# Gaps behind streamed weight blocks: where the matmul's moving operand begins within 512 bytes

## The reference

```python
h = rms_norm_2(x, attn_norm[l])
proj = h @ w_in[l]                         # 3648 columns
...                                        # three attention mixers
x = x + mixed @ w_o[l]
h = rms_norm_2(x, mlp_norm[l])
x = x + jnp.square(jax.nn.relu(h @ w_up[l])) @ w_down[l]   # 8192 wide
```

## Time and profile before

| | |
|---|---|
| Median of three runs | 3000.07 us |
| The profiled execution's own time | 3000.52 us |
| Its span | 2998.7 us |
| TensorE busy (matmul) | 2876.8 us, 96% of the span, 13692 matmuls |
| TensorE busy (weight load) | 2424.2 us, 81% |
| VectorE, ScalarE busy | 1878.9 us (63%), 1478.9 us (49%) |
| Loaded by SyncE's queue | 600.42 MB in 170912 packets, 59.3% of 16 engines |

### The profile page before, as it was taken

How to read it: one execution, slowest core, us unless ns; L and a number is a source line. 1 busy time by engine, 2 the same in 40 slices (tenths; PEclk the granted TensorE clock), 3 DMA queues, 4 the chain that set the end, 5 groups by cost and what they waited for, 6 DMA issues and landing times.

```text
span 2998.7 us, 35050 instructions
## 1 busy us (share of the span) xinstructions
PE 2876.8 (96%) x13692; PEld 2424.2 (81%) x13692; DVE 1878.9 (63%) x2387; ACT 1478.9 (49%) x2038; POOL 48.5 (2%) x60
## 2 busy tenths in 40 slices
PE   5998997999999999999999999999999999999998
PEld 4886776888888888788888888888887888888887
DVE  7997998669855557655444554545566554445554
ACT  4446544565546655644334444455546443344443
POOL 0000000000000000000000000000000000000000
PEclk9999998999999999999999999999999999999999
DMA  9994687757654544455555555555445555655654
GB/s 381 341 351 166 222 312 287 271 180 252 229 174 157 175 139 153 171 185 187 190 195 190 184 188 191 182 179 163 140 157 172 186 189 190 192 189 187 201 192 140
DMA packets 173045, 609.66 MB, mean 203 GB/s; under 512 B 19360, under 2 KB 19632, under 8 KB 172240
## 3 DMA queue, kind: packets, MB, share of 16 engines
q1 hardware_dynamic: 170912, 600.42, 59.3%
q0 software_dynamic: 1824, 6.61, 0.8%
q10 hardware_dynamic: 144, 0.39, 0.0%
HBM read 605.24 MB, written 2.10 MB: 203 GB/s over the span
## 4 chain that ended last, share of the span: by engine, by line
PE 83%; DVE 8%; ACT 4%; DMA 3%; issue 2%; SPq 0%; POOL 0%; POOLq 0%; ACTq 0%; DVEq 0%
PE ps L1908 26%; PE ps L1911 25%; PE ps L1915 25%; DVE w_lo L1214 2%; PE ps L1867 2%; DVE raw L1322 1%; PE ps L2033 1%; PE ps L2017 1%; ACT w_hi L876 1%; PE ps L1925 1%; DMA raw<-in_w_ina 1%; ACT probs L1078 1%; DMA raw<-in_w_modT 1%; DMA raw<-in_w_in 0%; DMA raw<-in_w_inc 0%
## 5 line engine op out<-in xcount | busy, mean ns | idle before, releaser
L1214 DVE TENSOR_TENSOR w_lo<-raw,w_hi 128x1024 fp32r<-128x1024 f32 (+4 forms) x988 | 1158.1, 1176 | 967.7 <-ACT w_hi L876 963.7
L876 ACT ACTIVATE w_hi<-raw 128x1024 fp32r<-128x1024 f32 (+4 forms) x988 | 1003.1, 1019 | 1229.2 <-PE ps L1915 1061.8
L1908 PE MATMUL ps<-w_hi,hT_hi 128*128 128x512 f32 (+3 forms) x2848 | 764.0, 390 | 35.2 <-ACT hT_hi L957 18.6
L1911 PE MATMUL ps<-w_lo,hT_hi 128*128 128x512 f32 (+3 forms) x2848 | 740.2, 382 | 0.8 <-DVE w_lo L1214 0.8
L1915 PE MATMUL ps<-w_hi,hT_lo 128*128 128x512 f32 (+3 forms) x2848 | 736.8, 380 | 0.0
L1908 PEld LDWEIGHTS ps<-w_hi,hT_hi 128*128 128x128 f32 x2848 | 519.7, 190 | 126.4 <-issue 25.5
L1911 PEld LDWEIGHTS ps<-w_lo,hT_hi 128*128 128x128 f32 x2848 | 535.1, 190 | 91.7 <-DVE w_lo L1214 1.1
L1915 PEld LDWEIGHTS ps<-w_hi,hT_lo 128*128 128x128 f32 x2848 | 534.3, 189 | 89.2
L1908 PE MATMUL ps<-w_hi,uT_hi 128*128 128x512 f32 x1024 | 275.7, 390 | 0.0
L1911 PE MATMUL ps<-w_lo,uT_hi 128*128 128x512 f32 x1024 | 274.4, 389 | 0.0
L1915 PE MATMUL ps<-w_hi,uT_lo 128*128 128x512 f32 x1024 | 274.4, 389 | 0.0
(11 more groups left out here) (246 smaller groups left out, 1476.1 us busy)
## 6 DMA issues: line engine op xcount, KB each, us to landing
raw<-in_w_up SPq DMA_DIRECT2D x256, 512.0 KB, 3.4
raw<-in_w_down SPq DMA_DIRECT2D x256, 512.0 KB, 3.4
raw<-in_w_modT SPq DMA_DIRECT2D x192, 512.0 KB, 5.5
raw<-in_w_rest SPq DMA_DIRECT2D x80, 456.0 KB, 3.3
raw<-in_w_z SPq DMA_DIRECT2D x64, 512.0 KB, 4.5
raw<-in_w_out SPq DMA_DIRECT2D x64, 512.0 KB, 4.5
raw<-in_w_rest SPq DMA_DIRECT2D x48, 344.0 KB, 3.5
raw<-in_w_oa SPq DMA_DIRECT2D x32, 512.0 KB, 3.4
```

The lines of the kernel that those rows point to most:

```text
L876: act.activation(w_hi[:, L % SPLIT_SLOTS, 0:c, 0:w], blocks(raw, G % RAW_SLOTS, c, w), ACT.Copy).then_inc(S.hi_ready, 1)
L1214: dve.tensor_tensor(blocks(w_lo, r, c, w), blocks(raw, r, c, w), w_hi[:, s, 0:c, 0:w].bitcast(F32), ALU.subtract).then_inc(S.group_read, 1)
L1908: pe.matmul(o, rows(hi, c, t), wh[c], start=start and c == 0, stop=False)
L1911: pe.matmul(o, rows(hi, c, t), wl[:, c], start=False, stop=False)
```

## The change

Each `raw` slot gets 4 unused words behind it (16 bytes), and each block of `w_hi` gets 16 (64 bytes). The places that used a whole slot now name its first 1024 words. Nothing else is edited, but what is allocated behind `raw` moves: `w_hi` by 160 bytes, `hf` and the work area by 672 (160 + 512).

```diff
+RAW_SHIFT = 4
+SHIFT = 16
...
-        raw = sb("raw", [P, RAW_SLOTS, GROUP])
-        w_lo = at("w_lo", [P, RAW_SLOTS, GROUP], F32R, cursor[0] - 4 * RAW_SLOTS * GROUP)
+        raw = sb("raw", [P, RAW_SLOTS, GROUP + RAW_SHIFT])
+        w_lo = at("w_lo", [P, RAW_SLOTS, GROUP + RAW_SHIFT], F32R, cursor[0] - 4 * RAW_SLOTS * (GROUP + RAW_SHIFT))
...
-        w_hi = sb("w_hi", [P, SPLIT_SLOTS, GROUP // COLS, COLS], F32R)
+        w_hi = sb("w_hi", [P, SPLIT_SLOTS, GROUP // COLS, COLS + SHIFT], F32R)
...
-                w = raw[:, G % RAW_SLOTS]
+                w = raw[:, G % RAW_SLOTS, 0:GROUP]
...
-                w = raw[:, G % RAW_SLOTS:G % RAW_SLOTS + 2].rearrange("p s n -> p (s n)")
-                dve.scalar_tensor_tensor(out=w, in0=w, scalar=1.0, in1=c_row[:].rearrange("p a n -> p (a n)"),
+                w = raw[:, G % RAW_SLOTS:G % RAW_SLOTS + 2, 0:GROUP]
+                dve.scalar_tensor_tensor(out=w, in0=w, scalar=1.0, in1=c_row[:],
```

## The result

The changed kernel takes 3043.89 us (median of four runs, 3039.1 to 3045.24), the kernel before 2999.68 on the same chip. The ratio is 1.0143, 95% interval 1.0131 to 1.0155: 1.4% slower, 44 us between the medians. Forecast were 3021 us, with 3007 to 3040 as the forecast's own range and 2935 to 3060 over all cases. The direction held, the amount is twice the forecast one.

The account below looks back on a forecast made before the run. Behind a DMA-paced opening of 225 us, TensorE's matmul step was taken as the bound. 3000.52 us plus 20.5 for 512-wide matmuls, all else 0, gave 3021.0, or 3021 at the runs' median; range 3007 to 3040, over all cases 2935 to 3060.

Parts of the forecast that it names:

- The bound, and the place of the change: Behind the first 225 us, time is the number of matmuls times their step; the 512-wide matmuls' step is what changes.
- The excess of 13.4 ns: Each 512-wide matmul's step over 213.3 ns of array time, taken as TensorE's moving-block and next-stationary-piece reads of SBUF meeting.
- The price per matmul, +2.3 ns: Each of 8892 512-wide matmuls was to take 2.3 ns longer from off-grid starts, +20.5 us in all.
- 344's +6: At width 344, each of the two matmuls off the 512 grid was read as 6 ns longer.
- the unsettled 230: Behind a TensorE pause, aligned blocks take 230 ns each before settling at 226.7; the 3.3 ns difference was noted above +2.3.
- The stationary side: The prediction noted that `uT` moves to 160 bytes past the grid while `hT` stays on it, with no separate price.
- Gaps on ScalarE and VectorE 0: Writing `w_hi` with a gap between its two runs was to cost 0; idle time would hide any step.
- Landings 0: DMA landings off the grid in the first 225 us were taken as 0, with +28 us as the other end.
- Widths 344 to 456 at 0: Some 2900 matmuls of these widths already mix offsets, so the change was to cost them 0.
- Rival 1: Fewer meetings of TensorE's two reads with many offsets, so a smaller excess and a faster kernel: 2970 us, chance 0.33.
- Rival 3: Varied offsets keep TensorE often in the worst phases: +6 ns for each of 8892 matmuls, +56 us, 3056; chance 0.06.
- The signs named: In the "down" products, durations should spread from 389/389/389, median near 391, and four matmuls take 0.91 to 0.93 us.

## Why the prediction was right and wrong

- The bound, and the place of the change: right. TensorE's step sets the time, and 40.8 to 44 of 44.3 us are 512-wide matmuls.
- The excess of 13.4 ns is TensorE's own and comes and goes with the phase of two reads: right as far as it is TensorE's own (alone it is 226.7 too). That one of the two is the data of the next weight load is not borne out, since 2 stationary columns leave 15.6 to 18.3 ns. The stationary piece's start counts; making the piece smaller doesn't lower the excess.
- The price per matmul, +2.3 ns: this step failed. It measured 44 us / 8892 = 5.0 ns. I averaged what off-grid starts did at widths 344 and 456 (2.0) and how far 450 and 456 lie above the settled 512 (2.4 and 2.6). The last two say nothing about starts: alone, with every block aligned, 450 columns take 203.3 ns, just the 203.3 of the earlier trace rows, and 456 take 208.9, 18.9 over the array time.

```profile
374.44 7.57 PE L137 MATMUL ps<-fill 128*128 128x450 f32 x36
381.85 0.30 PE L138 MATMUL ps<-fill 128*128 128x64 f32 x2
```

The 2.0 rests mostly on 344's +6, and 344 alone and aligned settles at 157.8 in one repetition and at 153.3 in the other. So these widths don't settle at 13.4 over even when aligned, and their off-grid blocks had little to lose; what 512 has to lose is its settled state. The trace before had the better row: the unsettled 230 of the earlier trace rows, 3.3 ns, which I named and set aside. Taken over the whole trace, the 871 steps of 512 columns other than 226 or 227 ns average 231.7, and with their neighbours counted in 230.6: 4.9 or 3.8 ns more than the settled step, +34 to +44 us. That is worked out after the fact, but from the trace before alone.
- The stationary side: I let "uT moves to 160 past the grid" stand and gave it no price. Alone it costs 23 us. The starts should have been tabulated against `hT` and `uT` separately.
- Gaps on ScalarE and VectorE 0: right (1058 and 1224 ns for 1024 elements). Landings 0: the opening 225 us moved 350 GB/s against 358, but 353 and 354 also in kernels that leave `raw` alone, and the longer matmuls account for the whole difference; no cost of landings is shown.
- Widths 344 to 456 at 0: nearly. 450 rose from 203.6 to 205.2 and 344 from 155.3 to 157.4, together 2.4 us.
- Rival 1 (fewer meetings), which got 0.33, rested on the idea that an average start is better than the aligned one. None that was measured is better than the aligned one. Rival 3's mark, medians over 394, was met in the low term of the down products (396) without its 56 us: the other two terms lie lower there, with means of 393.
- The signs named: the spread came (387 to 403), the median was 396, not 391, and four matmuls take 0.92 to 0.94 us.

## What to carry to other kernels

Where float32 (fp32r) blocks are streamed through TensorE at full clock, keep the start of the moving block and that of the stationary piece equal modulo 256 bytes: here it is worth 5 ns of 232 for each 512-column matmul, and a pad of 256 is free where one of 64 costs 1.1%. With 512 columns this was tried at equal starts of 0, 64 and 160. Anything allocated in front of them can break it, so the start of the area is as much a part of the layout as the pads. If a trace shows hundreds of matmuls of one and the same duration, that regularity is something that the kernel has and can lose; the same trace's unsettled matmuls, taken all together, give a first price.

## What the runs showed of the hardware

- With the stationary piece on the grid, the step of a 512-column float32 matmul at 2.4 GHz depends on the moving start modulo 256 bytes: 226.7 ns at 0, 228.9 at 64, 230 to 234.7 at the other multiples of 16 up to 224, 236.7 at 240 and at 4. Moving both by 64 or 160 bytes gives 226.7 again, but the difference of the starts is not all: a stationary start of 240 alone leaves 226.7, where the difference gives 231.7. At 1.2 GHz nothing of it is seen: 425 ns for 512 columns before, and a mean of 426.4 ns over 42 such steps in the changed kernel.
- Disturbed, a line of aligned matmuls alone took up to ten of them to settle, once with steps of 235, 233, 236, 224, 231, 236, 228, 233 and 231 ns, then 226.7 for good. Starts that change keep the ones on the grid from it too: 230.6 ns with the gaps in raw.
- A moving operand of 512 float32 columns with a stride of two words takes (16.28 - 0.50) / 35 = 451 ns, twice as long (the first step is 0.50 us):

```profile
69.01 16.47 PE L61 MATMUL ps<-fill 128*128 128x512 f32 x36
85.29 0.32 PE L62 MATMUL ps<-fill 128*128 128x64 f32 x2
```

- The Trainium skill's "SBUF — State Buffer", section "A bandwidth-pool intuition that's wrong (but worth ruling out)", gives the load of weights a second, independent read port beside that of the moving operand. The runs with TensorE alone show that the stationary start matters to the step all the same: moving the stationary piece alone by 160 bytes takes the step from 226.8 to 233.3 ns. What couples them stays open.
